# A decoder layer on one core: the residual returned in three pieces, the last two columns by halves of the tokens, and the first rows stored under them

## The reference, cut to what matters

```
xn = rmsnorm(h, g_mix);  q, k, v, u = split(xn @ w_in)
h = h + concat(attention(q, k, v), pool_mixer(u)) @ w_out
gate, up = split(rmsnorm(h, g_ffn) @ w_gate_up)          # 2 x 5632 columns
h = h + (silu(gate) * up) @ w_down                       # 5632 -> 2048
h = h + sigmoid(rmsnorm(h, g_ple) @ w_ple_gate) * (p_i @ w_ple_proj)
y = rmsnorm(h, g_final)                                  # stored, 520 rows of 2048
```

## Time and profile before

| what | us |
|---|---|
| median of 3 runs | 2353.88 (2353.14 to 2356.29) |
| the profiled execution | 2355.11 |
| its span | 2353.3 |
| TensorE products busy | 2271.7 (97%) |
| VectorE busy | 1637.1 (70%) |
| ScalarE busy | 1075.0 (46%) |
| GpSimd busy | 189.8 (8%) |

### The profile page before, as it was taken

The page is one execution under the profiler, slowest core; times in us unless marked ns, Lnnn a source line. Parts: engine busy times, 40 slices in busy tenths (PEclk is TensorE's granted clock), DMA queues, the critical chain, the costliest instruction groups (busy, mean ns, idle before and its releaser), DMA issues.

```text
span 2353.3 us, 45755 instructions
## 1 busy us (share of the span) xinstructions
PE 2271.7 (97%) x18543; PEld 2221.0 (94%) x18543; DVE 1637.1 (70%) x2116; ACT 1075.0 (46%) x1621; POOL 189.8 (8%) x87
## 2 busy tenths in 40 slices
PE   7999999999999999999999999999899999989995
PEld 6988898888999999999999999999899999979995
DVE  5355655564257888888888888888677777884332
ACT  5334454443245554544445454544444444564432
POOL 0031112201221000000000000000000000121110
PEclk9999999999999999999999999999999999999998
DMA  7455565543335445454545455457956775423322
GB/s 253 139 159 160 164 199 180 166 122 127 93 89 158 128 135 162 130 167 139 170 139 170 139 157 152 135 162 248 296 155 169 230 193 159 134 77 97 104 81 73
DMA packets 487664, 359.41 MB, mean 153 GB/s; under 512 B 8321, under 2 KB 469202, under 8 KB 486649
## 3 DMA queue, kind: packets, MB, share of 16 engines
q1 hardware_dynamic: 470457, 345.15, 49.5%
q10 hardware_dynamic: 17112, 12.95, 1.7%
HBM read 301.23 MB, written 57.29 MB: 152 GB/s over the span
## 4 chain that ended last, share of the span: by engine, by line
PE 90%; DVE 4%; DMA 2%; ACT 1%; issue 1%; SPq 1%; POOL 0%; ACTq 0%; DVEq 0%; POOLq 0%
PE acc L1130 39%; PE acc L687 30%; PE scores L1130 15%; PE scores L687 2%; PE mail_bank L687 1%; PE o_bank L687 1%; DVE w_low L2269 1%; DVE w_low L1823 1%; DMA region<-in_x_prompt 1%; DVE x_low L1831 1%; DMA x_low<-act_low_rows 0%; DMA key_pages<-in_w_down 0%; PE mail_bank L851 0%; SPq L621 0%; ACT w_high L1293 0%
## 5 line engine op out<-in xcount | busy, mean ns | idle before, releaser
L1130 PE MATMUL acc<-x_high,w_high 128*128 128x260 f32 x1584 | 449.5, 284 | 12.8 <-DVE w_low L2269 10.3
L1130 PE MATMUL acc<-x_low,w_high 128*128 128x260 f32 x1584 | 448.2, 283 | 0.0
L1130 PE MATMUL acc<-x_high,w_low 128*128 128x260 f32 x1584 | 448.0, 283 | 0.0
L687 PE MATMUL acc<-x_high,w_high 128*128 128x260 f32 x2048 | 432.5, 291 | 10.8 <-DVE w_low L1823 6.1
L687 PE MATMUL acc<-x_high,w_low 128*128 128x260 f32 x2048 | 416.8, 284 | 0.0
L687 PE MATMUL acc<-x_low,w_high 128*128 128x260 f32 x2048 | 416.8, 284 | 0.0
L2269 DVE TENSOR_TENSOR w_low<-raw,w_high 128x1024 fp32r<-128x1024 f32 (+4 forms) x252 | 285.7, 1134 | 121.5 <-ACT w_high L1619 120.5
L687 PEld LDWEIGHTS acc<-x_high,w_high 128*128 128x128 f32 x2048 | 319.0, 191 | 33.5 <-issue 24.2
L2269 DVE TENSOR_TENSOR w_low<-key_pages,w_high 128x1024 fp32r<-128x1024 f32 (+4 forms) x252 | 283.5, 1132 | 88.5 <-ACT w_high L1619 87.7
L687 PEld LDWEIGHTS acc<-x_low,w_high 128*128 128x128 f32 x2048 | 319.3, 190 | 0.1
L687 PEld LDWEIGHTS acc<-x_high,w_low 128*128 128x128 f32 x2048 | 319.2, 190 | 0.0
(11 more groups left out here) (293 smaller groups left out, 4000.8 us busy)
## 6 DMA issues: line engine op xcount, KB each, us to landing
raw<-in_w_gate_up SPq DMA_DIRECT2D x44, 1024.0 KB, 6.3
key_pages<-in_w_gate_up SPq DMA_DIRECT2D x44, 1024.0 KB, 7.4
raw<-in_w_in SPq DMA_DIRECT2D x32, 1024.0 KB, 7.3
act_high_rows<-late_rounded SPq DMA_DIRECT2D x22, 910.0 KB, 5.3
act_low_rows<-late_rounded SPq DMA_DIRECT2D x22, 910.0 KB, 6.9
key_pages<-in_cache_k SPq DMA_DIRECT2D x32, 512.0 KB, 5.9
late<-in_cache_v SPq DMA_DIRECT2D x32, 512.0 KB, 6.0
raw<-in_w_out SPq DMA_DIRECT2D x16, 1024.0 KB, 6.0
```

The costliest lines, as they stand in the source:

```text
L687: return pe.matmul(o, l, r, start=start, stop=stop)
L1130: return pe.matmul(bank, w, x, start=start and first, stop=last, skip_group_check=True)
```

## The change

Three edits (in the diff, the first `half_column` and `finish` are ScalarE's, the last `half_column` is VectorE's). The DMA that brings the residual back becomes three (tiles 5 to 7, 8 and 9, 10 to 15), and operands of group 1 and pieces are interleaved with the weights in another order; VectorE waits for a piece at windows 3, 5 and 6. Columns 14 and 15 leave the loop and are computed as four half columns: column 14 and 15 for tokens 0 to 255, then both for tokens 256 to 519 (`quarter`). After the first two, the root, reciprocal and scaling of blocks 0 and 1 follow, each block stored in two halves of the channels; ScalarE issues the stores of blocks 0 and 2, SyncE those of 1, 3 and the samples. The last squares are not added by GpSimd: TensorE adds them into the sums. Square roots of a constant are executed at two places and a sigmoid at one.

```diff
+def quarter(i):
+    s, a = i % 2, i // 2
+    return s, a, (slice(0, 2 * P), slice(2 * P, T))[a], (2 * P, T - 2 * P)[a]
...
+            def load_h(i):
+                tiles = slice((5 * T, 8 * T, 10 * T)[i], (8 * T, 10 * T, KD * T)[i])
+                sp.dma_start(late[:, tiles], h_spill[:, tiles]).then_inc(h_back[i], 16)
...
+                if n == NS + 4:
+                    for i in range(2, 5):
+                        load_operand(1, i)
+                    load_h(1)
+                    load_operand(1, 5)
+                elif n == NS + 5:
+                    load_operand(1, 6)
+                    load_h(2)
                 if n == NS + 2:
                     store_act(FF // 2 - 1, FF)
                     sp.wait_ge(act_stored, 32 * (FF // 2))
-                    sp.dma_start(late[:, KEPT:], h_spill[:, KEPT:]).then_inc(h_back, 16)
-                if n == NS + 3:
-                    for i in range(4):
-                        load_operand(1, i)
-                if n == NS + 4:
-                    for i in range(4, 7):
+                elif n == NS + 3:
+                    load_h(0)
+                    for i in range(2):
                         load_operand(1, i)
...
+            for n, (b, k) in enumerate(((1, 0), (1, HK), (3, 0), (3, HK))):
+                sp.wait_ge(S["y_scaled"], n + 1)
+                sp.dma_start(y_rows(b, k), y_cells(b, k)).then_inc(S["y_stored"], 16)
...
-            with pe.Fori(1, KD // 2) as j:
+            with pe.Fori(1, KD // 2 - 1) as j:
                 ple(j)
-            turn_y(KD - 1, 1)
-            pe.wait_ge(S["pool_summed"], KD * 3)
-            pe.wait_ge(S["proj_free"], KD)
-            for b in range(4):
-                mm(sc[:, 0, b:b + 1], sum_sq[:, b * P:(b + 1) * P], ones[:, 0:1])
-            mm(sc[0:NB, 0, 4:5], sum_sq[:, SEQ:T], ones[:, 0:1]).then_inc(S["fin_stats"], 1)
...
+            for i in range(4):
+                if i < 2:
+                    begin(Slab(PLE_N + KD - 2 + i), PLE_T + KD - 2 + i)
+                half_column(i, range(HK))
+                if i == 0:
+                    turn_y(KD - 3, 1)
+                else:
+                    half_turn(i - 1)
+                half_column(i, range(HK, HK + 4))
+                if i == 2:
+                    pe.wait_ge(S["pool_summed"], KD * 2 + KD)
+                    row_sums(sum_sq, (0, 1), True, True).then_inc(S["fin_stats"], 1)
+                elif i == 3:
+                    pe.wait_ge(S["pool_summed"], KD * 2 + KD + 1)
+                    row_sums(sum_sq, (2, 3, 4), True, False)
+                half_column(i, range(HK + 4, KD)).then_inc(S["acc_ready"], 1)
+                half_projection(i)
+            half_turn(3)
+            pe.wait_ge(S["squared"], KD * 2 + KD + 2)
+            row_sums(sq[1], (2, 3, 4), False, True).then_inc(S["fin_stats"], 1)
...
+            def half_column(i):
+                s, a, tokens, n = quarter(i)
+                m, done = KD - 2 + s, KD - 2 + i + 1
+                tile = h_all[:, m, tokens]
+                act.wait_ge(S["acc_free"], PLE_T + done)
+                act.activation(silu_row[s][:, tokens], gate_row[s][:, tokens], ACT.Sigmoid).then_inc(S["silued"], 1)
+                if i == 3:
+                    act.activation(fin[:, 7:8], eps, ACT.Sqrt, scale=1.0 / D, bias=eps)
+                act.wait_ge(S["pool_summed"], KD * 2 + m - 1)
+                act.wait_ge(S["h_done"], done)
+                act.activation(hg_row[s][:, tokens], tile, ACT.Copy,
+                               scale=gains[:, m + V_FINAL:m + V_FINAL + 1]).then_inc(S["hg_ready"], 1)
+                act.activation(sq[s][:, tokens], tile, ACT.Square).then_inc(S["squared"], 1)
+                if i == 1:
+                    act.activation(fin[:, 5:6], eps, ACT.Sqrt, scale=1.0 / D, bias=eps)
...
+            def finish(a):
+                act.wait_ge(S["fin_stats"], a + 1)
+                for b in ((0, 1), (2, 3, 4))[a]:
+                    n = NB if b == 4 else P
+                    act.activation(fin[0:n, b:b + 1], fin_sums[b], ACT.Sqrt, scale=1.0 / D,
+                                   bias=eps[0:n, :]).then_inc(S["fin_root"], 1)
+                if not a:
+                    act.activation(fin[:, 6:7], eps, ACT.Sigmoid)
+                act.wait_ge(S["fin_inv"], 2 * a + 1)
+                act.wait_ge(S["y_taken"], KD + 2 * a)
+                for k in (0, HK):
+                    A.step(act.activation(y_cells(2 * a, k), y_cells(2 * a, k), ACT.Copy, scale=fin[:, 8 + 2 * a:9 + 2 * a]))
+                    A.wait()
+                    act.dma_start(y_rows(2 * a, k), y_cells(2 * a, k)).then_inc(S["y_stored"], 16)
+            half_column(0)
+            half_column(1)
+            finish(0)
+            half_column(2)
+            half_column(3)
+            finish(1)
...
-                    if v == 3:
-                        dve.wait_ge(h_back, 16)
+                    if v in (3, 5, 6):
+                        dve.wait_ge(h_back[v // 2 - 1], 16)
...
+            def half_column(i):
+                dve.wait_ge(S["acc_ready"], PLE_T + done)
+                V.says(tt(gate_row[s][:, tokens], acc[s][:, a, 0:n], rstd[:, tokens], ALU.mult), S["acc_free"], PLE_T + done)
+                dve.wait_ge(S["proj_ready"], done)
+                dve.wait_ge(S["silued"], FF + done)
+                V.says(tt(up_row[:, tokens], sc[:, s, 0:n], silu_row[s][:, tokens], ALU.mult), S["proj_free"], done)
+                V.wait()
+                tt(h_all[:, m, tokens], h_all[:, m, tokens], up_row[:, tokens], ALU.add).then_inc(S["h_done"], 1)
```

More of the change, by code:

```diff
@@ L447, in layer @@
         act_stored = sem("act_stored")
-        h_back = sem("h_back")
+        h_back = [sem(f"h_back{i}") for i in range(3)]
         op_landed = [sem(f"operand_landed{i}") for i in range(7)]
@@ L1275, in _, with half_column @@
             turn_y(0, 0)
-            with pe.Fori(1, KD // 2) as j:
+            with pe.Fori(1, KD // 2 - 1) as j:
                 ple(j)
-            turn_y(KD - 1, 1)
-            pe.wait_ge(S["pool_summed"], KD * 3)
-            pe.wait_ge(S["proj_free"], KD)
-            for b in range(4):
-                mm(sc[:, 0, b:b + 1], sum_sq[:, b * P:(b + 1) * P], ones[:, 0:1])
-            mm(sc[0:NB, 0, 4:5], sum_sq[:, SEQ:T], ones[:, 0:1]).then_inc(S["fin_stats"], 1)
+            def half_column(i, ks):
+                s, a, tokens, n = quarter(i)
+                for k in ks:
+                    w_high, w_low = wh[s][:, k * P:(k + 1) * P], wl[s][:, k * P:(k + 1) * P]
+                    for c, (w, x) in enumerate(((w_high, xh), (w_high, xl), (w_low, xh))):
+                        ins = mm(acc[s][:, a, 0:n], w, x[:, k, tokens], start=k == 0 and c == 0, stop=k == KD - 1 and c == 2)
+                return ins
@@ new lines, in half_projection @@
+            def half_projection(i):
+                s, a, tokens, n = quarter(i)
+                pe.wait_ge(S["wp_low"], KD // 2)
+                pe.wait_ge(S["proj_free"], KD - 2 + max(i - 1, 0))
+                for k in (0, 1):
+                    at = k * 2 * P + s * P
+                    w_high, w_low = act_h[:, 2, at:at + P], act_l[:, 2, at:at + P]
+                    for c, (w, x) in enumerate(((w_high, act_h), (w_high, act_l), (w_low, act_h))):
+                        ins = mm(sc[:, s, 0:n], w, x[:, k, tokens], start=k == 0 and c == 0, stop=k == 1 and c == 2)
+                ins.then_inc(S["proj_ready"], 1)
@@ new lines, in half_turn @@
+            def half_turn(i):
+                s, a, tokens, n = quarter(i)
+                pe.wait_ge(S["hg_ready"], KD - 2 + i + 1)
+                pe.wait_ge(S["y_taken"], KD - 2 + i)
+                for b in (2 * a, 2 * a + 1):
+                    ins = pe.transpose(mbank[:, b * P:(b + 1) * P], hg_row[s][:, b * P:(b + 1) * P], ident)
+                if a:
+                    ins = pe.transpose(obank[0:NB, 0:P], hg_row[s][:, SEQ:T], ident)
+                ins.then_inc(S["y_turned"], 1)
@@ new lines, in row_sums, with add @@
+            def row_sums(squares, blocks, start, stop):
+                def add(out, rows):
+                    return pe.matmul(out, rows, ones[:, 0:1], start=start, stop=stop, skip_group_check=True)
+                for b in blocks:
+                    ins = add(fin_sums[b], squares[:, b * P:min((b + 1) * P, T)])
+                return ins
+            for i in range(4):
[15 more added lines that the diff above has]
+                half_projection(i)
@@ L1804, in _ @@
[L1804 to L1813, removed]
+            def half_column(i):
+                s, a, tokens, n = quarter(i)
+                m, done = KD - 2 + s, KD - 2 + i + 1
[11 more added lines that the diff above has]
+                    act.activation(fin[:, 5:6], eps, ACT.Sqrt, scale=1.0 / D, bias=eps)
+                act.wait_ge(S["squared"], KD * 2 + done)
+                act.wait_ge(S["y_turned"], done)
+                if a:
```

(35 more changed lines are left out.)

19 lines of the change are left out of this document (9 added, 10 removed).

## The result

The changed kernel takes 2342.76 us (median of 5, 2341.69 to 2344.21) against 2355.05 (2353.14 to 2356.29) for the kernel before, timed beside it: ratio 0.9948, 95% interval 0.9936 to 0.9961, so 12.3 us less, 9 to 15 by the interval. The forecast was 14.7 us less. The profiled execution took 2344.21 us, its span is 2342.4.

A forecast was written before the change was run, and what follows sets the result against it. TensorE's products are 90% of the chain, so only its waits and the tail can give time back: 7.8 + 6.9 = 14.7 us off the runs' median of 2353.88, 2339.2; range 2334.5 to 2347.0.

The forecast's parts named there:

- first stall: Near 1683 us, TensorE waits 8.6 us for the fifth visit's weights, queued behind the residual; with slow products, 11.0 us go.
- new wait for operand 6: Last product of the fifth visit waits for operand 6, now behind the sixth weights: 2.3 us, ends 0 and 4.5.
- At 311 GB/s they land at: SyncE's queue at the earlier mean rate: fifth weights land at 1671.3, operand 5 1686.7, sixth weights 1693.4, operand 6 1696.8.
- No wait at the start of the fifth visit: First weights' split ends at about 1677.4, TensorE's fourth visit at 1677.6; the third product's split perhaps 0.4 us late.
- The clock: After each new TensorE wait, half of the 1.8 us that a halved clock costs is charged: 0.9 us.
- The tail: Columns 14 and 15 as four half columns: wait of 2.2 us before half 2's turn, yet the end 6.9 us earlier.
- part 1: Residual in three pieces, around the fifth visit: 11.0 - 2.3 - 0.9 = 7.8 us gained; ends 11.0 and 4.7.
- (a): Rival: neither new wait bites, at the fifth visit or in the tail; 19.5 us gained, 2334.4; chance 12%.
- (d): Rival: queued pieces share the engines evenly, fifth weights land no sooner than 1683; only 6.9 us gained, 2347.0; chance 6%.
- (b): Rival: both new waits at their long ends, clock at half after each; 4.7 + 4.0 = 8.7 us gained, 2345.2; 20%.
- (c): Rival: ScalarE's table switches in the tail cost a drain, 2.6 us in all; 12.1 us gained, 2341.8; chance 5%.
- (e): Rival: TensorE's instruction supply stops in the written-out last columns, twelve times 1.7 us; slower, 2359.6; chance 4%.

The follow-up runs named there:

- e1: Kernel before with only the new order in SyncE's queue (residual in three pieces) and VectorE's three waits; ratio 0.9978 to the kernel before.
- e5: Changed kernel with block 0 scaled on VectorE and stored by SyncE instead of both on ScalarE; ratio 0.9943 to the kernel before.
- e6: Changed kernel without the three activations on constants that load ScalarE's tables early; ratio 0.9961 to the kernel before.
- e7: Changed kernel with e4's edit, and operand 2 of group 1 issued ahead of the fifth visit's weights; ratio 0.9924 to the kernel before.
- e2: Changed kernel with the old DMA order and the one wait, so the tail edit alone; ratio 0.9962 to the kernel before.
- e3: Changed kernel with operand 6 issued ahead of the sixth visit's weights; ratio 0.9939 to the kernel before.
- e4: Changed kernel with operands 0 and 1 of group 1 issued before the wait for the last activation store; ratio 0.9945 to the kernel before.

## Why the prediction was right, and which terms were off

**Place and cause of the first stall: right.** The weights of the fifth visit landed 9.8 us earlier in the trace, the 8.6 us wait and the slow 24 products behind it went. e1 shows that this part alone does it.

**The new wait for operand 6: right in kind, mis-sized.** The step that failed is "At 311 GB/s they land at", with operand 6 at 1696.8, and with it "I take 2.3. Its ends are 0 and 4.5": the landing was 1699.56, the wait 5.2, outside the ends. The upper end was added up wrongly too: 10% less bandwidth adds at least 4.5 us to the 45.1 up to operand 6, on top of the 1.9 of wait that were there, so it is 6.4 or more, not 4.5; what was measured is 7% less. With the same order of the queue the four profiles have 5.2 (changed), 4.2 (e1), 2.8 (e5) and 3.3 (e6), so 3.9 on average, and a HEAD of 76.7 on average: 6.3 us gained, not 7.8.

Why 288 and not 311: 3.1 of the 3.6 us are lost by the landing of the fifth weights already (1673.6, from a queue that began 0.8 us sooner than forecast, against 1671.3), and the slices put the loss at the queue's head. The mean rate of before had 2.93 MB of residual in it, the fastest bytes there (389 and 489 GB/s in the earlier trace rows); of these the change puts 1.6 MB behind operand 6, so what is ahead of it is slower than the mean. Also, "in order" is not strict: when operand 6 had landed, 14.75 MB had moved by the trace's packets, 0.7 of them from the piece of residual behind it. These are readings of slices and packets; none was tested by itself, and why the four profiles of one order differ by 2.4 us in this wait is open. The pause at 1649 to 1652 is no part of it, since the forecast's sum begins behind it; it is a reserve, which e7 uses.

**No wait at the start of the fifth visit: nearly.** 0.7 us, then 0.35 us at the third product, near the 0.4 that the text left to the next term. (The sixth weights' "4.1 us after landing" are 4.4 by the prediction's own times; nothing hangs on it, since they landed at 1695.8 and TensorE was held by operand 6.)

**The clock: the half was fair, as a mean.** Behind the wait for operand 6 the 48 products take 7.83 us (changed, wait 5.2), 7.53 (e1, 4.2), 7.53 (e5, 2.8) and 5.99 (e6, 3.3). From the chain and the stretches of e5, then of e6:

```profile
1692.98 7.53 PE acc L1161 x48
...
1694.00:1696.00 2.00, 2.00 (x11) 2.00 (x10) 2.00 (x5) 0.00 (x0) 0.00 (x0) 0.50 0.92 336
```

```profile
1696.63 5.99 PE acc L1161 x48
...
1698.00:1700.00 2.00, 2.00 (x19) 2.00 (x18) 2.00 (x4) 0.21 (x1) 0.00 (x0) 1.00 0.93 321
```

So the clock costs 1.8, 1.5, 1.5 and 0 there, where the forecast had 0.9 for a wait of 2.3. The wait of 1.99 us in the tail occurs alike in the changed kernel, e2, e3, e4 and e7: TAIL is 45.5 in three of them and 47.0 and 47.1 in e2 and e7, where 12 products behind it take 2.64 us. So it costs either nothing or 1.5, by the execution, and which of the two a profile shows is chance.

**The tail: right, nearly term by term.** Wait before half 2's turn 2.2 forecast, 1.99 measured; products' end to first scaling 4.7 against 4.9; from there to the end of the stores' 10.2 against 10.2 (2332.2 to 2342.4). From the start of column 14 to the last products' end 29.8 us, where before had 25.5: 4.3 more, against 3.9 and 0.9 of clock, which this profile did not pay. The gain was 7.2 in this profile, where 6.9 were forecast; over the five profiles of the same tail (45.5, 47.0, 45.5, 45.5, 47.1) it is 6.6. With the 6.3 of part 1 that makes 12.9, against the 12.3 of the medians. That ScalarE's order makes the wait is shown by e5; the drain that the Trainium skill's page "ScalarE: Activation LUTs", section "What ACT_TABLE_LOAD costs", gives a switch of tables (some 1,380 ns beside the load) is in none of the rows read here (e6, where the root follows 0.01 us after the load).

**The rivals.** (a) and (d) are out by the waits and landings. (b) had 4.7 us for the first part, and the profiled execution's was 4.4, with its long wait and low clock. (c) gave 12.1 us in all, next to the measured 12.3, but this is chance: e6's rows show no drain. (e) has no sign: the four half columns run at 2.82 to 2.91 us for 24 products.

## What to carry to other kernels

When a transfer is taken out from ahead of another in a full queue, redo the sum of bytes for every later landing, with a rate for each kind of rows (here 233 to 279, 356 to 364 and up to 489 GB/s in these two kernels) and not with the mean, and look for semaphores at which the issuing engine will now stand with an empty queue: filling those pauses (e7) brought another 5.6 us by the medians' ratios. Filling one pause of two (e4) brought nothing that can be told from scatter. An order of two transfers that are both late only chooses the waiter (e3). On a kernel whose executions scatter by several us (2350.4 to 2358.6 for the kernel before in one set), compare stretches between two fixed products too, but keep several profiles of the unedited stretch beside them: here it scatters by 4.3 us, and one profile of e3 or e4 against one of the changed kernel would have said more than is so.

## What the runs showed of the hardware

A wait of TensorE of about 2 us (1.99) left the granted clock at 1.00 in three profiles (changed, e3, e4) and took it to 0.50 in two others (e2, e7) of the same instructions, at a price of 1.5 us. At the first visit waits of 2.4 (before), 2.2 (e7), 2.7 (e4) and 2.6 us (e6) were followed by 24 products in 4.67, 4.66, 4.40 and 3.14 us. For operand 6, 3.3 us of waiting left it at 1.00 (e6) and 2.8 us took it to 0.50 (e5). The length of the wait alone does not say whether the clock falls.

DMAs of the same kind and size (weights in rows of 512 B) ran at 263 to 279 GB/s at one place and at 233 to 241 at another 20 us later in the same execution; the cause is open.

A DMA issued behind another on SyncE's queue moved 0.7 MB before the other had landed (the last piece of the residual behind operand 6, in the changed kernel).

A load of ScalarE's table took 1.28 us, began within 0.02 us of the end of the instruction before it and was followed by its root within 0.02 us (e6: 2329.38, 2330.67).
